# A wait before the first layer's ranked expert pieces, until all token rows are scattered

## What is computed

```python
s = sigmoid(t @ w_router)                 # t: the layer's tokens, 16 affinities each
sel = s + b_router
grp_score = sum of the two best sel of each of 4 groups
eidx = the two best experts inside the best group
wts = s[eidx] / sum(s[eidx])
for e in range(16):
    y = (silu(t @ w_gate[e]) * (t @ w_up[e])) @ w_down[e]
    out = out + combine[:, e:e + 1] * y
```

## Time and profile before

| | us |
|---|---|
| median of three runs | 1370.53 |
| the profiled execution's own time | 1371.52 |
| its span, first to last instruction | 1369.4 |
| TensorE busy | 1243.1 |
| DMA pieces of wexp, 190 of 1 MB, median from issue to landing | 15.4 |
| first layer's experts, from the first product | 486 |
| last layer's experts, from the first product | 1113 |

### The profile page before, as it was taken

One profiled execution on the slowest core, in us unless ns is written; L12 is line 12 of the kernel. 1 busy time (PEld: TensorE's weight loads), 2 busy tenths in 40 slices (PEclk: granted clock), 3 DMA queues, 4 the chain that ended last, 5 costly groups with the idle time before them and its releaser, 6 DMA issues.

```text
span 1369.4 us, 20046 instructions
## 1 busy us (share of the span) xinstructions
PE 1243.1 (91%) x8172; PEld 783.0 (57%) x8172; DVE 622.9 (45%) x1122; ACT 369.1 (27%) x599; POOL 124.5 (9%) x119
## 2 busy tenths in 40 slices
PE   4799999999999898999989957899999988998996
PEld 1577688787777633433333336787889833443443
DVE  2728467786464542211131127577876562221222
ACT  2523234442253310100100015544546420000000
POOL 0000000000022020000000020007930310000000
PEclk9999999999999999999999977999999999999998
DMA  9734469463635579999899982875354779999996
GB/s 380 292 134 198 167 246 383 132 223 123 246 123 219 215 277 343 339 355 354 307 373 401 414 315 110 334 314 213 124 154 154 309 290 367 399 387 398 398 420 250
DMA packets 59887, 382.73 MB, mean 279 GB/s; under 512 B 8912, under 2 KB 11412, under 8 KB 20308
## 3 DMA queue, kind: packets, MB, share of 16 engines
q1 hardware_dynamic: 45584, 345.00, 65.1%
q10 hardware_dynamic: 9748, 18.74, 4.2%
q0 software_dynamic: 4464, 17.71, 3.6%
HBM read 363.84 MB, written 44.84 MB: 298 GB/s over the span
## 4 chain that ended last, share of the span: by engine, by line
issue 22%; PE 19%; DMA 14%; DVE 6%; ACT 2%; POOL 2%; SPq 0%; DVEq 0%; POOLq 0%; ACTq 0%
DMA wexp<-in_expert 11%; PE bank L2045 3%; PE bank L2047 3%; PE bank L2046 3%; PE bank L2467 3%; DMA x_rows<-trow,rowid 2%; PE bank L2452 1%; PE bank L2013 1%; PE bank L2485 1%; POOL x_rows L782 1%; PE bank L2055 1%; POOL m_lo L766 1%; PE bank L2137 1%; DMA stage<-in_in 1%; PE bank L2325 1%
## 5 line engine op out<-in xcount | busy, mean ns | idle before, releaser
L2452 PE MATMUL bank<-wexp,xg 128*64 128x512 f32 (+1 forms) x1488 | 264.9, 598 | 12.4 <-DMA wexp<-in_expert 9.4
L2045 PE MATMUL bank<-h_hi,whi 128*128 128x512 f32 (+1 forms) x640 | 224.8, 351 | 15.9 <-DVE h_lo L1271 11.7
L2047 PE MATMUL bank<-h_hi,wlo 128*128 128x512 f32 (+1 forms) x640 | 219.6, 343 | 0.0
L2046 PE MATMUL bank<-h_lo,whi 128*128 128x512 f32 (+1 forms) x640 | 219.6, 343 | 0.0
L2452 PEld LDWEIGHTS bank<-wexp,xg 128*64 128x64 f32 (+1 forms) x1488 | 77.3, 125 | 164.3 <-issue 143.1
L2467 PE MATMUL bank<-wexp,act_a 128*32 128x256 f32 (+1 forms) x1072 | 150.6, 505 | 19.5 <-DMA wexp<-in_expert 15.3
L1271 DVE TENSOR_TENSOR wlo<-stage,whi 128x2048 fp32r<-128x2048 f32 x56 | 133.7, 2395 | 40.3 <-ACT whi L809 28.4
L2045 PEld LDWEIGHTS bank<-h_hi,whi 128*128 128x128 f32 x640 | 124.1, 194 | 40.0 <-issue 14.6
L1271 DVE TENSOR_TENSOR act_a<-act_s,bank 128x256 f32<-128x256 f32 (+1 forms) x47 | 17.2, 365 | 256.7 <-ACT act_s L809 256.7
L2046 PEld LDWEIGHTS bank<-h_lo,whi 128*128 128x128 f32 x640 | 123.9, 194 | 13.5 <-issue 0.5
L2047 PEld LDWEIGHTS bank<-h_hi,wlo 128*128 128x128 f32 x640 | 123.6, 193 | 13.7
(11 more groups left out here) (343 smaller groups left out, 1599.5 us busy)
## 6 DMA issues: line engine op xcount, KB each, us to landing
wexp<-in_expert SPq DMA_DIRECT2D x190, 1024.0 KB, 15.4
stage<-in_in SPq DMA_DIRECT2D x40, 1024.0 KB, 8.5
raw<-in_mod SPq DMA_DIRECT2D x18, 1024.0 KB, 7.0
stage<-in_mod SPq DMA_DIRECT2D x16, 1024.0 KB, 4.9
x_rows<-in_c_zero SPq DMA_DIRECT2D x32, 512.0 KB, 7.7
y_rows<-in_c_zero SPq DMA_DIRECT2D x20, 512.0 KB, 7.8
spare<-in_mod SPq DMA_DIRECT2D x8, 1024.0 KB, 16.9
stage<-in_out SPq DMA_DIRECT2D x8, 1024.0 KB, 4.8
```

The costliest lines, as they stand in the source:

```text
L2045: MM(o, w[0], x_[0], start=start, stop=False)
L2046: MM(o, w[0], x_[1], start=False, stop=False)
L2047: return MM(o, w[1], x_[0], start=False, stop=stop)
L2452: ins = MM(bank[0][g * w:(g + 1) * w, :], x_[:, 2 * j + k, :], weights[:, c], start=(first_ == 0), stop=(last_ == 0))
```

## The change

The condition under which SyncE waits for the scatters now also holds in the first layer. There it stands before piece 0 of the first ranked expert (rank 3), and the value is that of the first layer's own eight scatters. In the last layer place and value stay what they were. Nothing else is changed.

```diff
                     if plan.side and r == plan.aside and j < plan.side:
                         expert_unit(e, plan.slot[r], j, side[j][:, :], ("spare_a", "spare_b")[j])
                         continue
-                    if l == DEPTH - 1 and (r, j) == (plan.aside, plan.side):
+                    if (r, j) == ((plan.aside, plan.side) if l == DEPTH - 1 else (plan.loads[LEADERS[l]], 0)):
 
-                        sp.wait_ge(sem("all", "scattered"), sum(2 * (span(i) // P) for i in range(DEPTH)) * 16)
+                        sp.wait_ge(sem("all", "scattered"), sum(2 * (span(i) // P) for i in range(l + 1)) * 16)
                     if plan.uses_before(r, j) > 0:
                         sp.wait_ge(S(f"used{plan.slot[r]}{j}"), plan.uses_before(r, j))
                     expert_unit(e, plan.slot[r], j)
```

## The result

The changed kernel takes 1376.46 us, median of 10 runs (1373.12 to 1378.73), where the kernel before takes 1370.03 in 10 runs beside it (1366.03 to 1374.19): a ratio of 1.0045, 95% interval 1.0029 to 1.0060. So it is slower by 6.2 us, 4.0 to 8.2. The forecast was 1372.5, range 1368.0 to 1376.3 on the first median of 1370.53. The sign was right, but the forecast's plus 1.9 to 2.0 us is a third of what was measured, and the measured median lies 0.2 us above the upper end of the range (0.4 above it where the 6.2 us are added to the first median). The profiled execution took 1378.73 us, span 1376.6.

The account below looks back on a forecast made before the run. TensorE, busy 91% of the span, was taken as the bound; where edited, scatters and pieces share full DMA engines. Piece 5 late, plus 2.6, act_a minus 0.7: plus 1.9 on 1370.53, so 1372.5 us, range 1368.0 to 1376.3.

Parts of the forecast that it names:

- the stop for act_a: TensorE's 0.70 us wait at 544.93: y_rows written at about 527, down by 542, so minus 0.7 us.
- When the wait opens: SyncE, first layer: first ranked piece issued at about 503.5 instead of 488.09; bounds 503.3 and 505.
- The first four pieces: Rank 3's pieces read in step 2: pieces 1 to 3 land late, step 2 ends 2 us late, bounds 0 and 5.
- my discount for fewer xpick rows: Step 2: 2.9 us late by the last layer's rows, taken as 2 because xpick rows are 512 against 640 KB.
- The last two pieces: Rank 3's pieces 4 and 5, step 2's down product: piece 5 lands at 540.2, second half plus 2.6 us.
- The first sum: Piece 5's landing added up from release, ten pieces, xpick rows, constants and a y_rows write: 538.8, or 541.3 with more ahead.
- The 3.8 us for the xpick rows: Term in piece 5's landing: 512 KB of xpick rows cost 2.6 us beyond their own 1.2.
- The Trainium skill's port rule: Tiles of 32 or 64 partitions get at most half bandwidth: xpick term 2.4 us, piece 5 landing 1.4 us sooner.
- rival B: Clock falls in the new gap before step 2's down product: 1.7 us more, 1374.1 to 1377.2; chance 0.18.
- Rival A: Pieces keep up: piece 5 lands at 534 to 536, TensorE no longer waits, 1366.5 to 1369.5; chance 0.14.
- Rival D: Queues still behind at 560, steps 6 and 8 wait too: plus 1 to 3 more, 1374 to 1376; chance 0.06.
- the 3.27 us for xpick: TensorE's stop at 535.17 for the xpick rows goes, as they are issued at 503.7 instead of 527.5.

Follow-up runs that it names:

- the filler: Changed kernel plus matmuls whose result is never read, ahead of step 3's down product: with 16, 1383.91 us (1.0091 of the kernel before); with four, 1372.87 us (1.0012).

## Why the prediction was right, and why its size was not

In the main the wait and the late pieces were forecast rightly, and one step, the stop for act_a, was not; it carries most of the loss, with the clock that fell behind it.

*When the wait opens*: forecast 503.5, 4.4 us after the last scatter's issue; measured 504.59, of which 0.6 is GpSimd's later start, and 4.9 us. Right, 0.5 us short.

*The first four pieces*: forecast 515.9, 518.6 and 521.3, step 2 late by 2 (0 to 5); they came at 516.3, 518.7 and 521.9, and step 2 ended 3.3 us late. Within the bounds, nearer to the last layer's rows than to my discount for fewer xpick rows.

*The last two pieces*: piece 5 forecast at 540.2, landed at 539.81 (issued 513.14, 26.7 us to landing). The product's end plus 1.93 against a forecast of 2.6. The place was right, the sum partly by luck. Counted from SyncE's first issue piece 5 took 35.2 us, where the forecast had 36.7; that the wait opened 1.1 us late hid this. The first sum comes to 35.3 us from that issue, but with 3.6 us for the constants; with the constants out of piece 5's way it still landed 33.2 us after that issue (behind the write) and 33.9 (on SyncE), so they cost 1.3 to 2.0 us, and the other terms together were as much dearer as this was cheaper. The 3.8 us for the xpick rows are isolated by no run. The Trainium skill's port rule (SBUF — State Buffer, Door 1) gave an estimate of 538.8, which is 35.3 us after the forecast's opening; measured from the opening it is nearer than the 36.7, in absolute time farther off, so the landing decides nothing between row and rule. The stop before the second half was 1.73 us and there was none before the first, where the forecast had 3 to 4.5: step 2 was later than the 2 us taken, and piece 4 landed at 536.0, not 537.8.

*The stop for act_a*: this step failed. The prediction said that ScalarE "writes y_rows at about 527; the write is down by 542, so the 0.70 us goes too". It was issued at 528.7 and down at 547.8. I had counted the constants as bytes before piece 5, and y_rows as bytes too, but not that both go through one queue of ScalarE's, the constants first. The row for it lay there: in the kernel before ScalarE already waited 8.68 us for this very write, and I took that for a price that would fall when the write was issued sooner. It rose: the engines, half free from 540 to 544 then, were full now, and the queue in front of the write was the same. The term was minus 0.7; it measured plus 3.26.

*The clock* was rival B, with the right price (1.70 us, as in the earlier trace rows) at the wrong place: not at the down product of step 2, where TensorE stood still for 1.73 us, but at the next down product, after the gap that the forecast did not have. Forecast plus B's price and the stop make 1.93 + 3.26 + 1.70 = 6.89.

*Rival A* (the pieces keep up) did not happen. Its 30.8 us for piece 5 does not follow from the forecast's own numbers: the second half of the product could begin at 536.3 (534.5 and 1.8), which is 32.8 after 503.5; the measured 35.2 is over both. *Rival D* (a delay that is not made good after 560) did not either: plus 6.89 at step 6, plus 7.20 at step 26. *What it gives*: the 3.27 us for xpick did go, and TensorE stood elsewhere in its stead, more of it in step 2 (2.64 us) and less before the down product (1.73) than forecast.

That the write's place behind the constants makes the stop, and not the full engines alone, is shown by the constants' move within ScalarE's step, and again by the move to SyncE. It takes both: in the kernel before, the write stood behind the same constants on half free engines, and the stop was 0.70 us. That the late down pieces cost nothing beside it is shown by putting them first; and with the constants behind the write there is no stop for them at all. That the gap lowers the clock is shown by the filler. Not tried: the write of y_rows on another queue with everything else as it was, and a second buffer for yrow, which would take the wait away rather than shorten it.

## What to carry to other kernels

A transfer that is made to wait for another takes its turn later on full engines; before costing it, list all that will then stand in front of it and beside it, by queue and not only by bytes. A small write that an engine must see landed before it can go on doesn't belong behind a megabyte of loads that nobody needs soon: here that order cost more than the transfers that were held back. And a queue that waits for a buffer is a wait for everything behind it: here that order of issue gave the gap that an explicit wait was meant for, and the explicit wait added nothing to it.

## What the runs showed of the hardware that was not expected

A 256 KB write took 19.1 us from issue (528.71) to the end of the wait (547.80) behind 1.2 MB on its own queue, while a 1 MB piece on SyncE's queue issued at 526.52 landed 16.7 us later and the next, issued at 528.21, 19.5 us later. So the small write was as slow as a full piece with the pieces before it still in its way. A matmul of 128x512 in float32 that uses all 128 columns took 0.88 us (14.06 for 16; 0.93 with four), where the experts' products, which go to two halves of 64 columns, take 0.46 each. Gaps of 2.00 and 2.96 us on TensorE were followed by a slow product and gaps of 1.73 and 3.27 us were not, so the length of a gap alone does not tell.
